# Attention of two layers: copies ahead of exponentials, plain outputs scaled once per token tile, five selection rounds moved

## The chip, the cores and the metric

The program runs on one core of one Trainium2 chip, as one launch. The metric is the device time of one execution in microseconds (us). Five engines work side by side, each with its own queue of instructions and joined only by semaphores: TensorE (PE; its weight loads are listed as PEld), VectorE (DVE), ScalarE (ACT), GpSimd (POOL) and the DMA queues, here those of SyncE (SP) and of ACT.

## The reference, cut to what matters

The program computes one state-space and mixture-of-experts block and then two layers of the following form on 512 tokens of width 1024. The change touches only the attention inside these two layers.

```python
for layer in range(2):
    h = rms_norm(x, g_mix[layer])
    qa, ka, va, iq, ik, iw, qb, kb, vb = split(h @ w_in[layer])
    out_a = dsa_mixer(qa, ka, va, iq, ik, iw)      # "plain": softmax over the keys that an index picks
    out_b = diff_mixer(qb, kb, vb, lam, ...)       # "differential": softmax 1 - lam * softmax 2, then a norm
    x = x + concat(out_a, out_b) @ w_out[layer]
    x = x + (silu(h2 @ w_gate) * (h2 @ w_up)) @ w_down     # h2 = rms_norm(x, g_ffn)
```

`dsa_mixer` has 8 heads of 64 values. For each query the index scores the keys and the best 128 of them are kept: a round finds the 8 largest scores of each row (`max`) and takes them out (`match_replace`), so a tile of 128 queries needs 16 rounds. `diff_mixer` has 4 heads with two score matrices each and 128 values.

## The kernel before, in words

**Units.** The attention of a layer is 32 units, `UNITS = [(i, h, d) for d in (1, 0) for i in range(4) for h in range(4)]`. Units 0 to 15 are differential (diff) and 16 to 31 plain; `i` is the tile of 128 queries and `h` a head (diff) or a pair of heads (plain). Tile `i` sees `128 * (i + 1)` keys, so the units grow with `i`: units 0 to 3 and 16 to 19 have 128 keys, 12 to 15 and 28 to 31 have 512. Each unit has two score matrices, c = 0 and 1.

**The pipeline of a unit u.** `qk` (PE, L3334) writes both score matrices to banks 2(u%2) and 2(u%2)+1 of PSUM. `top` (DVE, L3440) adds the mask, takes the negative row maximum and writes them to `Pb[u % 4]`. The exponentials (ACT, L3390) work in place on `Pb`. `normal` (DVE) divides: a diff unit by a reciprocal and two `scalar_tensor_tensor` (L3452 to L3457) into one matrix, a plain unit by a reciprocal and two `tensor_scalar` (L3459, L3461, L3462). `tr` (PE, L3344) transposes the 128x128 pieces into banks 4 and 5, ACT copies them to `PTb[u % 4]` (L3399), `pv` (PE, L3354 diff, L3359 plain) multiplies by the values into bank 6 + u%2, and ACT copies the result out (L3405): diff to `ob`, tokens on partitions; plain straight into `ym`, features on partitions, because there the values are the stationary operand with 64 columns and the transposed probabilities move.

**Order of work.** No planner is used: each engine runs a hand-written loop over steps s. PE at step s issues qk(s), tr(s-3), pv(s-4). ACT issues exp(s), copy(s-3), out(s-4). DVE issues top(s), at most one item of the rest of the key choice, normal(s-2), and some extras. The rest of the key choice is 17 items of the list `IDX`: a `bias` of tile 2 at s = 0, 15 rounds of tile 3 at s = 1 to 15, the `bias` of tile 3 at s = 16 (`index_dve`, rounds L3258 and L3260, bias L3262 to L3266). The bias of tile 3 is read first by top(28). Extras of DVE: `squares` of tile 0 to 3 at s = 21 to 24 (with the sums `n_sum` at 24), two splits of weights at s = 25 and 26 (L2942), a reciprocal at s = 27, the scaling of `ob` at s = 28 to 31 (L3502). Extras of ACT: two splits at s = 17 and 18 (L2938), the square root for the norm at s = 25 (L3412), which loads a function table and makes the next exponential load its own again.

**What waits.** qk(u) waits for top(u-2), tr(u) for normal(u) and for copy(u-1), pv(u) for copy(u) and for out(u-2), top(u) for qk(u) and tr(u-4).

**The end.** PE transposes `ob` into banks 0 to 3 at s = 33 and 34 (L3374) and ACT scales and copies it into `ym[4:8]` (`rows_T`, L3383). Then for k = 0 to 7 ACT rounds `ym[k]` to `hx[0]` (L3420) and DVE writes the remainder to `hx[1]` (L3505); ahead of k = 4 ACT splits one more weight item. The output projection (`lout_pe`, products at L296 to L298) takes its 1024 rows in pairs kp = 0 to 3 for the first half of columns; pair kp waits for the remainders of k = 2kp and 2kp+1. The load of the ring slot that holds `ym` waits for the remainder of k = 7 (`layers_sp`). After that PE runs through the output projection and the feed-forward part.

## Time and profile before

| what | before |
|---|---|
| runs, us | 3008.04, 3013.76, 3015.8 |
| median, us | 3013.76 |
| profiled execution: its time, us | 3006.61 |
| profiled execution: span in the trace, us | 3004.5 |
| mean granted clock of PE | 0.962 |
| attention, layer 0: first top to first product of the output projection | 1785.54 to 1892.75 us |
| attention, layer 1: the same | 2480.30 to 2586.05 us |

The profiled execution's own time is 2.1 us above its span. Times of rows are from the start of the span. The granted clock is 1.00 at 2.4 GHz and 0.50 at 1.2 GHz. The busy time of a row can overlap the next one by some ten nanoseconds, so that the cost of an instruction in a full queue is the distance from its start to the next start. An `[idle before <-X]` at the end of a row is the time for which the engine sat idle and what released it. An `xN` merges N instructions in a row; a 32-bit matmul is listed as two passes, a transpose as one.

### The profile page before, as it was taken

Reading aid. Unit: us, or ns where it says so; the run is one execution under the profiler, and the core shown is the slowest. Engines: PE = TensorE matmul, PEld = TensorE weight load, DVE = VectorE, ACT = ScalarE, POOL = GpSimd, SP = SyncE. Lnnn points to the kernel's source line nnn. Section 1 sums busy time; section 2 is a strip of 40 time slices with the busy share of each in tenths; the row PEclk is TensorE's granted clock in tenths of the full one; section 3 lists DMA queues with packets and bytes.
Section 4 is the critical chain, followed back from the end, with each engine's and each line's share of the span. In section 5 each row is a group of like instructions: output and inputs, shape, how many; then the busy total and the mean of one; then the engine's idle time right before and its main releaser. Section 6 shows DMA issues by size and latency. Waiting matters only on the chain.

```text
span 3004.5 us, 41883 instructions
## 1 busy us (share of the span) xinstructions
PE 2773.1 (92%) x16866; PEld 2113.7 (70%) x16866; DVE 1781.0 (59%) x3266; ACT 1137.6 (38%) x2028; POOL 152.4 (5%) x139
## 2 busy tenths in 40 slices
PE   7998977888999999999988987999999996899998
PEld 4887765776666676666645764788888774788887
DVE  4257866665777777766646698433333589443333
ACT  3322233222155655556523336432223336532222
POOL 0000000000012221222200000000000000000000
PEclk9998888989999999999999989999999998999999
DMA  6210001414269888999975320223313320222412
GB/s 226 85 57 22 1 1 48 123 53 154 98 245 355 337 346 328 343 358 348 361 291 206 106 97 1 86 90 107 110 67 121 110 103 8 85 70 78 140 53 74
DMA packets 186541, 442.37 MB, mean 147 GB/s; under 512 B 21283, under 2 KB 110694, under 8 KB 167014
## 3 DMA queue, kind: packets, MB, share of 16 engines
q1 hardware_dynamic: 161862, 396.59, 36.7%
q0 software_dynamic: 18720, 33.60, 2.9%
q10 hardware_dynamic: 5760, 9.44, 0.9%
q8 instruction: 136, 2.23, 0.3%
q14 instruction: 63, 0.52, 0.1%
HBM read 426.43 MB, written 38.29 MB: 155 GB/s over the span
## 4 chain that ended last, share of the span: by engine, by line
PE 65%; DVE 10%; DMA 6%; ACT 3%; issue 2%; POOL 0%; ACTq 0%; SPq 0%; POOLq 0%; DVEq 0%
PE ps L296 15%; PE ps L298 15%; PE ps L297 15%; PE ps L2496 5%; DMA ring<-in_ew 3%; DMA hg<-h_rows,idx 2%; PE ps L2012 2%; PE ps L1504 2%; DVE Pb L3440 1%; PE ps L2522 1%; PE ps L2735 1%; PE ps L2216 1%; DVE bi L3260 1%; DMA yr<-y_rows 1%; PE ps L3359 1%
## 5 line engine op out<-in xcount | busy, mean ns | idle before, releaser
L2942 DVE TENSOR_TENSOR wf<-ring,wf 128x1024 fp32r<-128x1024 f32 (+1 forms) x152 | 181.6, 1196 | 310.2 <-ACT wf L2938 309.9
L2938 ACT ACTIVATE wf<-ring 128x1024 fp32r<-128x1024 f32 (+1 forms) x152 | 156.8, 1033 | 342.9 <-PE ps L298 342.9
L296 PE MATMUL ps<-hxh,wf 128*128 128x512 f32 (+1 forms) x736 | 279.9, 380 | 2.3 <-DVE hxl L3089 2.3
L297 PE MATMUL ps<-hxl,wf 128*128 128x512 f32 (+1 forms) x736 | 279.5, 380 | 0.0
L298 PE MATMUL ps<-hxh,wf 128*128 128x512 f32 (+1 forms) x736 | 279.5, 380 | 0.0
L2434 DVE TENSOR_TENSOR spA<-ring,spA 128x1024 fp32r<-128x1024 f32 x156 | 184.4, 1221 | 103.8 <-ACT spA L2429 103.6
L2496 PE MATMUL ps<-ring,hdT 128*128 128x512 f32 x520 | 236.7, 598 | 0.8 <-issue 0.8
L2429 ACT ACTIVATE spA<-ring 128x1024 fp32r<-128x1024 f32 x156 | 157.9, 1054 | 50.5 <-DMA ring<-in_ew 44.3
L2434 DVE TENSOR_TENSOR spB<-ring,spB 128x1024 fp32r<-128x1024 f32 x104 | 124.1, 1220 | 69.3 <-ACT spB L2429 69.1
L2496 PEld LDWEIGHTS ps<-ring,hdT 128*128 128x128 f32 x520 | 94.5, 192 | 95.5 <-issue 92.0
L296 PEld LDWEIGHTS ps<-hxh,wf 128*128 128x128 f32 x736 | 138.4, 188 | 29.0 <-DVE hxl L3089 2.8
L297 PEld LDWEIGHTS ps<-hxl,wf 128*128 128x128 f32 x736 | 138.4, 188 | 26.2
L298 PEld LDWEIGHTS ps<-hxh,wf 128*128 128x128 f32 x736 | 138.4, 188 | 25.9
L296 PE MATMUL ps<-wf,hhh 128*128 128x512 f32 x352 | 137.0, 389 | 0.0
L298 PE MATMUL ps<-wf,hhl 128*128 128x512 f32 x352 | 136.9, 389 | 0.0
L297 PE MATMUL ps<-wf,hhh 128*128 128x512 f32 x352 | 136.9, 389 | 0.0
L296 PE MATMUL ps<-hxh,wr 128*128 128x512 f32 (+1 forms) x320 | 125.4, 392 | 10.6 <-DVE wr L2942 7.4
L296 PE MATMUL ps<-spA,hgT 128*128 128x512 f32 x312 | 126.7, 406 | 2.3 <-DVE hgT L2570 2.3
L298 PE MATMUL ps<-hxh,wr 128*128 128x512 f32 (+1 forms) x320 | 125.7, 393 | 0.0
L297 PE MATMUL ps<-hxl,wr 128*128 128x512 f32 (+1 forms) x320 | 124.3, 389 | 0.0
L2429 ACT ACTIVATE spB<-ring 128x1024 fp32r<-128x1024 f32 x104 | 106.5, 1052 | 46.5 <-DMA ring<-in_ew 36.4
L297 PE MATMUL ps<-spA,hgT 128*128 128x512 f32 x312 | 123.7, 396 | 0.0
(616 smaller groups left out, 6161.4 us busy)
## 6 DMA issues: line engine op xcount, KB each, us to landing
ring<-in_ew SPq DMA_DIRECT2D x65, 2048.0 KB, 12.1
ring<-in_ew SPq DMA_DIRECT2D x65, 1024.0 KB, 6.7
ring<-in_w_in SPq DMA_DIRECT2D x17, 2048.0 KB, 7.9
ring<-in_w_gate SPq DMA_DIRECT2D x20, 1024.0 KB, 5.4
ring<-in_w_up SPq DMA_DIRECT2D x20, 1024.0 KB, 8.0
ring<-in_w_down SPq DMA_DIRECT2D x16, 1024.0 KB, 5.1
adaw<-in_ada_w SPq DMA_DIRECT2D x24, 512.0 KB, 6.3
ring<-in_w_out SPq DMA_DIRECT2D x6, 2048.0 KB, 9.7
```

Source lines behind the costliest of these rows:

```text
L296: pe.matmul(o, lhs[0], rhs[0], start=start, stop=False)
L297: pe.matmul(o, lhs[0], rhs[1], start=False, stop=False)
L298: return pe.matmul(o, lhs[1], rhs[0], start=False, stop=stop)
L1504: m = pe.matmul(o[half(c), 64 * h:64 * h + 64], l[half(c), 64 * h:64 * h + 64], r[half(c), 64 * h:64 * h + 64])
L2012: m = pe.matmul(ps[2 * (i % 2) + hf][:, :], ym[:, k, i * 128:(i + 1) * 128], wv[:, k, :], start=(k == 0), stop=(k == 5))
L2216: m = pe.matmul(b[:, t], sw13[:, k, 256 * q + f * 128:256 * q + f * 128 + 128], hT[:, k, t], start=(k == 0), stop=(k == 7))
L2429: act.activation(piece(e, j)[0], piece_raw(e, j), ACT.Copy).then_inc(*p_hi.inc((e, j)))
L2434: v.tensor_tensor(piece(e, j)[1], piece_raw(e, j), f(piece(e, j)[0]), ALU.subtract).then_inc(*p_lo.inc((e, j)))
L2496: m = pe.matmul(ps[5 + q][:, :], hdT[:, n % 2, j, :], w2[:, j, q * 512:(q + 1) * 512], start=(j == 0), stop=(j == 1))
L2522: m = pe.transpose(ps[q][:, j * 128:(j + 1) * 128], hg[:, n % 3, (q * 4 + j) * 128:(q * 4 + j + 1) * 128], ident)
L2938: act.activation(item_part(n)[0], item_raw(n), ACT.Copy).then_inc(*w_hi.inc(n))
L2942: v.tensor_tensor(item_part(n)[1], item_raw(n), f(item_part(n)[0]), ALU.subtract).then_inc(*w_lo.inc(n))
```

## The change

Four things are altered in the attention of both layers.

1. **Order on ACT.** At step s ACT issues copy(s-2), out(s-4), exp(s) in place of exp(s), copy(s-3), out(s-4). On DVE normal(s-1) takes the place of normal(s-2). PE keeps qk(s), tr(s-3), pv(s-4), with tr of a plain unit waiting for its exponentials alone.
2. **Plain outputs.** The plain probabilities are no longer divided. `normal` of a plain unit is one reciprocal, kept in a new tile `rin`. `pv` of a plain unit has the transposed probabilities (128 columns) as stationary operand and moves 64 columns of values; the four units of a token tile fill one bank, 6 + i%2, tokens on partitions. Once per tile DVE multiplies the bank by the reciprocals into `r1` (`plain_norm`), PE transposes four pieces back into the bank (`plain_T`), and ACT copies it to `ym[0:4]` (`plain_y`). The 16 copies of plain units (L3405) go. The first `pv` of tile i waits for the bank: for out(14 + i) if i < 2, else for `plain_y(i - 2)`.
3. **Key choice.** The 17 items are issued at the steps marked in `REST`: the bias of tile 2 at 0, rounds at 1 to 6, 8, 10, 12, 14 (10) and at 16 to 20 (5), the bias of tile 3 at 26.
4. **The end.** The rounding to `hx` goes in the order k = 4 to 7, then 0 to 3 (`YK`), and the first half of the output projection takes its pairs in the order 2, 3, 0, 1 (`KP`). The third weight split stands ahead of k = 0. Tile 3's `plain_norm`, `plain_T`, `plain_y` come after the loop.

```diff
+            rin = sb("rin", [128, 16, 2], c=s1)
...
+    KP = ((2, 3, 0, 1), (0, 1, 2, 3))
+    YK = (4, 5, 6, 7, 0, 1, 2, 3)
...
+    REST = [int(s in (0, 1, 2, 3, 4, 5, 6, 8, 10, 12, 14, 16, 17, 18, 19, 20, 26)) for s in range(34)]
...
             if m == 9:
-                sp.wait_ge(*y_lo.val((l, 7)))
+                sp.wait_ge(*y_lo.val((l, YK[7])))
...
         def tr(u):
-            pe.wait_ge(*u_nrm.val((l, u)))
+            pe.wait_ge(*(u_nrm if diff else u_exp).val((l, u)))
...
         def pv(u):
-            if u >= 2:
+            if diff and u >= 2:
                 pe.wait_ge(*u_out.val((l, u - 2)))
+            if not diff and h == 0:
+                pe.wait_ge(*(u_out.val((l, 14 + i)) if i < 2 else q_y.val((l, i - 2))))
...
-                        m = pe.matmul(ps[6 + u % 2][64 * c:64 * c + 64, 0:128], vt[:, j, 128 * h + 64 * c:128 * h + 64 * c + 64],
-                                      PTb[:, u % 4, c, j * 128:(j + 1) * 128], start=(j == 0), stop=(j == i))
+                        m = pe.matmul(ps[6 + i % 2][:, 128 * h + 64 * c:128 * h + 64 * c + 64], PTb[:, u % 4, c, j * 128:(j + 1) * 128],
+                                      vt[:, j, 128 * h + 64 * c:128 * h + 64 * c + 64], start=(j == 0), stop=(j == i))
+
+        def plain_T(i):
+            pe.wait_ge(*q_n.val((l, i)))
+            for h in range(4):
+                m = pe.transpose(ps[6 + i % 2][:, 128 * h:128 * h + 128], r1[:, i % 2, h * 128:(h + 1) * 128], ident)
+            m.then_inc(*q_T.inc((l, i)))
...
+            if s in (25, 29, 33):
+                plain_T((s - 25) // 4)
...
+        plain_T(3)
...
+        def plain_y(i):
+            act.wait_ge(*q_T.val((l, i)))
+            act.activation(ym_(l)[:, 0:4, i * 128:(i + 1) * 128], v4(ps[6 + i % 2][:, :]), ACT.Copy).then_inc(*q_y.inc((l, i)))
         for s in range(36):
+            if 2 <= s < 34:
+                i, h, diff = UNITS[s - 2]
+                act.wait_ge(*u_tr.val((l, s - 2)))
+                if s >= 6:
+                    act.wait_ge(*u_pv.val((l, s - 6)))
+                for c in range(1 if diff else 2):
+                    m = act.activation(PTb[:, (s - 2) % 4, c, 0:128 * (i + 1)], ps[4 + c][:, 0:128 * (i + 1)], ACT.Copy)
+                m.then_inc(*u_pt.inc((l, s - 2)))
+            if 4 <= s < 20:
+                act.wait_ge(*u_pv.val((l, s - 4)))
+                act.activation(ob[:, i, 128 * h:128 * h + 128], ps[6 + s % 2][:, 0:128], ACT.Copy).then_inc(*u_out.inc((l, s - 4)))
...
+            if s in (26, 30, 34):
+                plain_y((s - 26) // 4)
...
-        act.wait_ge(*u_out.val((l, 31)))
-        for k in range(8):
-            if k == 4:
-                act.wait_ge(*n_y.val((l, 3)))
+        rows_T(2)
+        act.wait_ge(*n_y.val((l, 3)))
+        for k in YK:
+            if k == 0:
+                act.wait_ge(*q_y.val((l, 3)))
                 split_hi(act, n0 + 2)
             act.activation(hx[0][:, k, :], ym_(l)[:, k, :], ACT.Copy).then_inc(*y_hi.inc((l, k)))
-            if k == 1:
-                rows_T(2)
+            if k == 5:
+                plain_y(3)
...
-                v.reciprocal(s_[:, 6:8], s_[:, 4:6]).then_inc(*V.inc())
-                v.wait_ge(*V.val())
-                v.tensor_scalar(p0, p0, s_[:, 6:7], None, ALU.mult).then_inc(*V.inc())
-                v.tensor_scalar(p1, p1, s_[:, 7:8], None, ALU.mult).then_inc(*u_nrm.inc((l, u)))
+                v.reciprocal(rin[:, u - 16, :], s_[:, 4:6]).then_inc(*u_nrm.inc((l, u)))
...
+        def plain_norm(i):
+            v.wait_ge(*u_pv.val((l, 19 + 4 * i)))
+            v.wait_ge(*u_nrm.val((l, 19 + 4 * i)))
+            if i >= 2:
+                v.wait_ge(*q_T.val((l, i - 2)))
+            v.tensor_tensor(r1[:, i % 2, :].rearrange("p (n q) -> p n q", q=64), ps[6 + i % 2][:, :].rearrange("p (n q) -> p n q", q=64),
+                            bc(rin[:, 4 * i:4 * i + 4, :].rearrange("p h c -> p (h c)"), 64), ALU.mult).then_inc(*q_n.inc((l, i)))
...
-            for x in rest[s:s + 1]:
+            for x in rest[at:at + REST[s]]:
                 index_dve(v, l, x)
-            if s >= 2:
-                normal(s - 2)
+            at += REST[s]
+            if 1 <= s < 33:
+                normal(s - 1)
...
+            if s in (24, 28, 32):
+                plain_norm((s - 24) // 4)
...
+        plain_norm(3)
+        for k in YK:
             v.wait_ge(*y_hi.val((l, k)))
...
+            for at, kp in enumerate(KP[hf][0:4 - 2 * hf]):
+                n = n0 + 4 * hf + at
```

## Rows read from the trace of the kernel before

**Rows 1.** Windows: us, busy us (instructions) of PE, PEld, DVE, ACT, POOL; clock; DMA.

```profile
1850.32:1892.75 42.43, 32.32 (x256) 22.39 (x257) 25.35 (x85) 29.09 (x77) 0.00 (x0) 0.96 0.00 1
2480.30:2527.80 47.50, 29.45 (x138) 16.75 (x136) 45.82 (x155) 24.85 (x89) 0.00 (x0) 0.75 0.04 12
2527.80:2545.20 17.40, 13.86 (x104) 9.44 (x104) 14.04 (x83) 13.82 (x54) 0.00 (x0) 1.00 0.01 2
2545.20:2586.05 40.85, 30.75 (x257) 21.76 (x257) 25.35 (x85) 28.92 (x77) 0.00 (x0) 1.00 0.00 1
```

**Rows 2.** Timeline, DVE, layer 1: start us, busy us, line, tiles, [idle before].

```profile
2520.35 0.68 DVE L3440 CUSTOM_DVE_ANT_0 Pb<-ps,zb 128x512 f32<-128x512 f32 x1
...
2521.57 0.69 DVE L3258 MAX8 m8b<-bi 128x8 f32<-128x512 f32 x1
...
2522.97 0.15 DVE L3452 RECIPROCAL stt<-stt 128x1 f32<-128x1 f32 x1
...
2524.08 0.68 DVE L3440 CUSTOM_DVE_ANT_0 Pb<-ps,zb 128x512 f32<-128x512 f32 x1
...
2528.22 0.42 DVE L3262 TENSOR_SCALAR bi<-bi 128x512 f32<-128x512 f32 x1
...
2529.32 0.16 DVE L3452 RECIPROCAL stt<-stt 128x1 f32<-128x1 f32 x1
```

**Rows 3.** Timeline, ACT, layer 1: around the square root, later units, the end.

```profile
2551.45 1.28 ACT L3412 ACT_TABLE_LOAD   x1
...
2554.36 0.61 ACT L3390 ACTIVATE Pb<-Pb,stt 128x384 f32<-128x384 f32 x1
...
2555.58 0.63 ACT L3399 ACTIVATE PTb<-ps 128x256 f32<-128x256 f32 x2
...
2560.24 0.72 ACT L3390 ACTIVATE Pb<-Pb,stt 128x512 f32<-128x512 f32 x1 [1.75 <-DVE stt L3440]
...
2561.67 0.84 ACT L3399 ACTIVATE PTb<-ps 128x384 f32<-128x384 f32 x2
...
2583.99 1.15 ACT L3420 ACTIVATE hxh<-ring 128x512 fp32r<-128x512 f32 x2
2585.05 1.25 ACT L3383 ACTIVATE ring<-ps,gsc 128x512 f32<-128x512 f32 x2
```

**Rows 4.** Timeline, DVE, layer 1, plain units.

```profile
2558.90 0.69 DVE L3440 CUSTOM_DVE_ANT_0 Pb<-ps,bi 128x512 f32<-128x512 f32 x1 [2.52 <-PE ps L3334]
...
2570.05 0.49 DVE L3461 TENSOR_SCALAR Pb<-Pb,stt 128x512 f32<-128x512 f32 x1
...
2570.85 0.68 DVE L3502 TENSOR_TENSOR ob<-ob,nrm 128x512 f32<-128x512 f32 x1
```

**Rows 5.** Groups by line and form, DVE, plain part of layer 1: busy us, mean ns.

```profile
L3472 DVE CUSTOM_DVE_ANT_0 nsq<-ob 128x128 f32<-128x128 f32 x16 | 3.7, 286 | 0.0
...
L3461 DVE TENSOR_SCALAR Pb<-Pb,stt 128x128 f32<-128x128 f32 x4 | 1.1, 286 | 0.1
```

**Rows 6.** Timeline, PE, layer 1.

```profile
2531.07 1.06 PE L3354 MATMUL ps<-vt,PTb 128*128 128x128 f32 x8
...
2557.72 1.13 PE L3334 MATMUL ps<-qT 64*128 64x512 f32 x4
2558.78 0.87 PE L3344 MATMUL ps<-csb,Pb 128*128 128x128 f32 x6
2559.59 1.14 PE L3359 MATMUL ps<-PTb,vt 128*64 128x128 f32 x12
...
2576.13 1.58 PE L3359 MATMUL ps<-PTb,vt 128*64 128x128 f32 x16
2577.64 1.09 PE L3374 MATMUL ps<-csb,ob 128*128 128x128 f32 x8
...
2586.05 0.47 PE L296 MATMUL ps<-wf,hxh 128*128 128x512 f32 x1 [2.40 <-issue]
```

**Rows 7.** Window of layer 0 inside the diff part, columns as in rows 1.

```profile
1804.00:1807.00 3.00, 2.77 (x12) 1.40 (x9) 2.90 (x11) 1.33 (x7) 0.00 (x0) 0.50 0.00 0
```

More of the change, by code:

```diff
@@ L382, in _program @@
     a_ada = Signal(sem("ada_mm"), range(4))
-    a_row = Signal(sem("ada_copy"), range(4))
-    a_rT = Signal(sem("ada_T"), range(2))
-    a_mod = Signal(sem("modc_set"), range(2))
+    a_row = Signal(sem("rows_copy"), range(4))
+    a_rT = Signal(sem("rows_T"), range(2))
+    a_mod = Signal(sem("rows_set"), range(2))
     SEGS = ((1, slice(0, 256)), (0, slice(256, 768)))
@@ L2884, in _program @@
         for hf in range(2):
-            add([krows(WO[:, hf * 512:(hf + 1) * 512])], 8, [("out", 0, A2[kp], slice(0, 512)) for kp in range(4)])
+            add([krows(WO[:, hf * 512:(hf + 1) * 512])], 8, [("out", 0, A2[kp], slice(0, 512)) for kp in KP[hf]])
         for grp in range(2):
@@ L2976, in _program @@
     u_pv = Signal(sem("unit_pv"), UL)
-    u_out = Signal(sem("unit_out"), UL)
+    u_out = Signal(sem("unit_out"), [(l, u) for l in range(2) for u in range(16)])
     i_mm = Signal(sem("index_mm"), IG)
@@ L2987, in _program @@
     lam_e = Signal(sem("lam_exp"), ["set"])
-    y_hi = Signal(sem("y_hi"), [(l, k) for l in range(2) for k in range(8)])
-    y_lo = Signal(sem("y_lo"), [(l, k) for l in range(2) for k in range(8)])
+    y_hi = Signal(sem("y_hi"), [(l, k) for l in range(2) for k in YK])
+    y_lo = Signal(sem("y_lo"), [(l, k) for l in range(2) for k in YK])
+    q_n = Signal(sem("rows_set"), [(l, i) for l in range(2) for i in range(4)])
+    q_T = Signal(sem("rows_T"), [(l, i) for l in range(2) for i in range(4)])
+    q_y = Signal(sem("rows_copy"), [(l, i) for l in range(2) for i in range(4)])
     o_tile = Signal(sem("tile_mm"), [(l, k, i) for l in range(2) for k in ("out", "ff") for i in range(3)])
@@ L3502, in attn_dve @@
                 v.tensor_tensor(v4(ob[:, i, :]), v4(ob[:, i, :]), bc(nrm[:, 0, 4 * i:4 * i + 4], 128), ALU.mult).then_inc(*n_mul.inc((l, i)))
-        for k in range(8):
+        plain_norm(3)
+        for k in YK:
             v.wait_ge(*y_hi.val((l, k)))
             v.tensor_tensor(hx[1][:, k, :], ym_(l)[:, k, :], f(hx[0][:, k, :]), ALU.subtract).then_inc(*y_lo.inc((l, k)))
-            if k == 3:
+            if k == 7:
                 split_lo(v, n0 + 2)
@@ L3514, in part @@
             for k in range(2):
-                kk, w = 2 * kp + k, item_part(n0 + 4 * hf + kp)
+                kk, w = 2 * kp + k, item_part(n0 + 4 * hf + KP[hf].index(kp))
                 m = mm3(pe, ps[4 * hf + i][:, :], [x[:, kk, i * 128:(i + 1) * 128] for x in hx], [x[:, k, :] for x in w],
-                        start=(kk == 0), stop=(kk == 7))
+                        start=(kk == 2 * KP[hf][0]), stop=(kk == 2 * KP[hf][3] + 1))
             return m
         for hf in range(2):
-            for kp in range(4 - 2 * hf):
-                n = n0 + 4 * hf + kp
+            for at, kp in enumerate(KP[hf][0:4 - 2 * hf]):
+                n = n0 + 4 * hf + at
                 pe.wait_ge(*w_lo.val(n))
@@ L3525, in lout_pe @@
                 for i in range(4):
-                    if hf == 0 and kp == 0:
+                    if hf == 0 and at == 0:
                         pe.wait_ge(*n_y.val((l, i)))
```

15 lines of the change are left out of this document (2 added, 13 removed).

## The prediction

> **What bounds the kernel now.** I read the windows first, cut at three marks: the first `top`, `top` of unit 16, `top` of unit 24, and the first product of the output projection. That gives part A (diff), B (plain, tiles 0 and 1) and C (plain, tiles 2 and 3, and the end). [rows 1] show A at 47.50 us with DVE busy for 45.82, so DVE alone sets A. In B (17.40 us) DVE is busy for 14.04 and in C (40.85) for 25.35, with PE at 30.75 and ACT at 28.92: there nobody is full and the engines wait for each other. Layer 0 has the same A and B and a C of 42.43. Behind C the PE products follow each other without a gap for most of the layer, so an earlier start of the output projection is an earlier end.
>
> The timelines then give the prices. In a full queue a price is the distance between starts; where only a busy time stands it is some 0.07 less. On DVE, at 512 keys [rows 2]: `top` 1.22, a round 1.40, `normal` of a diff unit 1.11, the bias of tile 3 1.10. A plain pair of multiplications costs 0.80 at 512 keys [rows 4] and, as 2 x 0.286 less overlap, 0.41 at 128 [rows 5]; 0.54 at 256 lies on the line. On ACT [rows 3]: two exponentials 1.22 at 384 keys and 1.43 at 512; two copies of transposes 0.55 at 256, 0.76 at 384 and so 0.95 at 512; a full-width copy 0.53 to 0.62; the square root with its two table loads 2.91. On PE [rows 6]: `qk` 1.06 at 512 keys; 6 transposes 0.81, 8 about 1.0; plain `pv` 1.07 at 384 keys (12 passes), 1.51 at 512 (16 passes). Waits: DVE sat 2.52 in front of top(28) [rows 4], behind the square root; ACT 1.75 in front of exp(28) [rows 3]; PE 2.40 before the output projection [rows 6], while ACT copied, rounded, and DVE took remainders.
>
> **Part A.** Of the 15 rounds ten stay and five leave: 5 x 1.40 = 7.0. normal(14) comes in, since `normal` runs one step earlier: + 1.1. Net 5.9 off, 41.6 left, if DVE stays the bound. A step without a round costs DVE 1.22 + 1.11 = 2.33 at 512 keys. Against that stand ACT with 1.43 + 0.48 + 0.17 = 2.1 and PE with 1.06 + 0.5 + 0.99 = 2.55 (`pv` 8 passes, [rows 6]); but steps with and without a round alternate, so DVE needs 3.0 on average. The longest circle that the new order makes is top, qk two steps on, tr, copy, exp, normal, top: 1.2 + 1.1 + 0.5 + 0.7 + 1.4 + 1.1 and some 0.5 of hand-overs, 6.5 in three steps, 2.2 a step. It is hidden.
>
> **Part B.** The diff part shows how full a full DVE queue looks: 45.82 / 47.50 = 0.965. So the 14.04 busy us of B are 14.5 of queue, and 2.9 were waiting [rows 1]. Out: the bias 1.1, normal(14) 1.1, six pairs of multiplications 4 x 0.41 + 2 x 0.54 = 2.7. In: five rounds 7.0, one more reciprocal 0.2. Sum 14.5 - 4.9 + 7.2 = 16.8. The 2.9 of waiting goes, because those waits were for PE held up by `copy`, and copy now stands ahead of exp; ACT and PE have some 14 us of work here. B falls by 0.6.
>
> **Part C**, as a timetable with t = 0 at top(24). DVE: top 1.0, squares 4 x 0.21 [rows 5] with three small sums 1.5, `plain_norm(0)` 0.6: done at 3.2. `plain_norm` has no row; the nearest is the 512-wide multiplication of L3502 with 0.68 busy, 0.60 in the queue [rows 4]. PE has reached `plain_T(0)` by then and waits in front of it, with qk(26) and tr(23) queued behind: transposes 0.5, qk 0.85, tr(23) 0.55, done at 5.1. This is the new wait. ACT holds exp(25) behind copy(23), so exp(25) ends at 7.0, square root and table loads 2.9, copy(24) 0.75, exp(26) 1.2: 11.8. `plain_y(0)` 0.6 ends at 12.4. DVE meanwhile does top(25), a split, top(26), the bias, a split, top(27) and waits some 2 us for exp(26); top(28) comes at 12.5. pv(24) is held by plain_y(0), its bank being in use, until 12.4; from there PE is full. Its list: pv(24) 1.07; three steps of qk, tr and pv, 1.06 + 0.81 + 1.07 each, of which the last has 8 transposes, + 0.2, and `plain_T(1)` 0.5: 9.5; tr(29), pv(28) 2.5; tr(30), pv(29), plain_T(2), eight transposes 4.0; tr(31), pv(30), eight transposes 3.5; pv(31) 1.5. Together 22.1, and one stall of 1.1: pv(28) needs plain_y(1), which stands behind copy(28) and exp(30). pv(31) ends at about 35.5. Then plain_norm(3) 0.7, and DVE's remainders of k = 4 and 5, 2 x 0.6, which alone keep the projection back; transposes and plain_y(3) go beside them. First product at 37.5. Against 40.85 that is 3.3 off in layer 1, and against 42.43, 4.9 in layer 0, where before one stretch ran at 0.96 of the clock.
>
> The other halves of the edit cost nothing on this path. The copies of 16 plain units (0.17 each) go off ACT. Pairs kp = 3, 0, 1 have 5.4 us of products each between them, and ACT's third split and the rest of the rounding need less. The ring load behind the last remainder moves with it. Should this cover fail, each late pair costs what it is late.
>
> **One price is unknown:** a pass with 128 stationary and 64 moving columns. 128 and 128 cost (1.06 - 0.07) / 8 = 0.124, 64 and 128 cost 1.51 / 16 = 0.094 [rows 6]. `qk` shows what moving columns cost: 1.06 / 4 = 0.265 at 512, and a straight line from 0.124 at 128 gives 0.03 for 64. So 0.124 - 0.03 = 0.094: no change, the value I take. Its bounds are 0.124 (moving fewer columns gives nothing) and 0.064 (the larger weight load costs nothing). PE is the bound for 112 passes of units 24 to 31 in each layer, so that is +-6.7 us over both layers. The Trainium skill ("TensorE: Matmul & The Clock Gate", section "LDWEIGHTS (loading the stationary operand)") has the load cost its columns at 1.2 GHz, 53 ns for the 64 added, which speaks against the swap: 0.094 + 0.053 - 0.03 = 0.117, + 5.2 us by an estimate from that page. The trace has the step from 64 to 128 stationary columns at 0.030, not 0.053.
>
> **Sum.** Layer 1: 5.9 + 0.6 + 3.3 = 9.8. Layer 0: 5.9 + 0.6 + 4.9 = 11.4. Together 21.2. The profiled execution took 3006.6 us, 2.1 above its span, and should take 2985.4. The median of the runs is 7.2 above that execution, and I keep this distance: 3013.8 - 21.2 = 2992.6.
>
> **Rivals.**
> 1. *The swapped product is dearer,* 0.124 a pass at worst. For it: no row has that form, and C is bound by PE. Against it: the line through its neighbours gives 0.094. Gain 21.2 - 6.7 = 14.5, time 2999. The page of the Trainium skill named above speaks for this rival, and would have it at 2998.
> 2. *Handing over eats it.* With DVE, ACT and PE all near 34 us in the 16 plain steps, any unevenness is a stall; the 2.9 of B come back and C loses as much again in waits such as plain_T in front of qk. Gain 21.2 - 2 x 5 = 11, time 3003. For it: C has both a filled PE and two waits of plain work on ACT. Against it: copy ahead of exp takes out the wait that ended most steps.
> 3. *PE at the lower clock becomes the bound of A.* A runs at 0.75 mean clock [rows 1], and at 0.50 PE was busy for 2.77 of 3.00 us just before the clock rose [rows 7]. With rounds gone, steps of tile 2 and 3 at 1.2 GHz need 3.2 and 4.4 to 5.0 of PE against 2.6 and 3.0 of DVE. If the clock stayed low to unit 16: + 8 a layer, gain 5, time 3009, no change by measure.
> 4. *The other side: the low clock lasts into the plain part.* Same place and mechanism. At 1.2 GHz a plain step of tiles 0 and 1 needs 2.7 to 3.8 of PE against about 2.1, 8 to 10 us in B, on top of rival 3. It decides once over 11 us of a layer's PE work that would have run at 2.4 GHz and is on the path runs at 1.2 beyond what did before: gain 5 - 18, time 3027. Against it: before, the clock rose as soon as PE had filled its queue, and the change fills it more.
> 5. *The load behind the remainders hides it:* no; PE waited for no weights in the feed-forward part.
>
> **How the numbers follow.** My forecast (gain 17 to 27) 0.58; rival 1 0.12; rival 2 0.16; rival 3 0.06; rival 4 0.04; better than that, by a cheap pass or better clock, 0.04. A measurement of this kernel tells 0.3%, 9 us, from no change. Faster: 0.58 + 0.12 + 0.12 of rival 2 + 0.04 = 0.86; same: the other 0.04 of rival 2 and 0.05 of rival 3; slower: 0.01 of rival 3 and 0.04 of rival 4. The range 2986 to 3003 takes in the forecast, rival 1 and half of rival 2.
>
> **What would show it.** A near 41.6 with DVE busy at 0.96 of it; B near 16.8 with no idle row over 0.5 at `top`; C near 37.5 in both layers; passes of L3359's successor near 0.094; PE full from pv(24) with about 1 us in front of pv(28); 0.7 to 1 us in front of the output projection. I am wrong if idle time appears on DVE in A, if PE waits for `plain_y` by more than named, if top(28) comes later than 13 behind top(24), or if the granted clock is 0.50 past unit 11.

## The result, and the profile after

Over six runs of each, side by side on one chip, the changed kernel's median is 2995.58 us (2987.31 to 2999.16) and that of the kernel before 3010.43 us (3006.31 to 3015.8). The ratio is 0.9945, its 95% interval 0.993 to 0.9959: faster by 0.55%. The forecast was 2992.6 us and a gain of 21.2; the medians give 14.9, the ratio 16.6. The direction and the range held. The gain is 5 to 6 us short, and the parts show where. That the time itself came within 3.0 us of the forecast is in part luck: the median of the kernel before, from which the forecast subtracts, is 3.3 us lower in these six runs than the 3013.76 that it started from.

| part, us | layer 0: forecast | before | after | layer 1: forecast | before | after |
|---|---|---|---|---|---|---|
| A: top(0) to top(16) | 41.6 | 47.37 | 41.57 | 41.6 | 47.50 | 41.56 |
| B: top(16) to top(24) | 16.8 | 17.41 | 15.49 | 16.8 | 17.40 | 15.60 |
| C: top(24) to the output projection | 37.5 | 42.43 | 41.07 | 37.5 | 40.85 | 42.49 |
| sum | 95.9 | 107.21 | 98.13 | 95.9 | 105.75 | 99.65 |

The table is from one profiled execution of each kernel. Together the two layers gain 9.08 + 6.10 = 15.2 us. The profiled execution of the changed kernel has a span of 2996.0 us, only 8.5 below that of before. The rest is ahead of the change: its first `top` starts at 1791.71 us, that of before at 1785.54, with the same code up to there. Over the profiles of this study that start lies between 1779.71 and 1791.71. So spans are not compared below, only the parts of the attention.

The windows of the changed kernel, A and B of layer 1, C of layer 0 and C of layer 1 (columns as in [rows 1]):

```profile
1848.77:1889.84 41.07, 35.66 (x261) 28.62 (x261) 21.13 (x71) 28.44 (x70) 0.00 (x0) 0.96 0.00 1
2476.30:2517.86 41.56, 30.30 (x154) 17.82 (x152) 40.02 (x142) 24.79 (x89) 0.00 (x0) 0.78 0.05 13
2517.86:2533.46 15.60, 13.51 (x102) 10.53 (x104) 15.34 (x83) 13.43 (x51) 0.00 (x0) 1.00 0.01 2
2533.46:2575.95 42.49, 36.98 (x261) 29.88 (x259) 21.09 (x71) 28.33 (x70) 0.00 (x0) 0.92 0.00 1
```

DVE is busy for 0.963 of A, about as before the change (0.965), and now for 0.98 of B. It has no idle row in either part. In C the granted clock is 0.96 in layer 0 and 0.92 in layer 1, against 0.96 and 1.00 in [rows 1].

The timeline of PE in C of layer 1 (it answers to [rows 6]) holds the shortfall:

```profile
2543.15 0.84 PE L3351 MATMUL ps<-csb,Pb 128*128 128x128 f32 x6
2546.24 2.79 PE L3368 MATMUL ps<-vt,PTb 128*128 128x64 f32 x12 [2.25 <-ACT ring L3404]
2548.97 2.08 PE L3341 MATMUL ps<-qT 64*128 64x512 f32 x4
2550.98 1.54 PE L3351 MATMUL ps<-csb,Pb 128*128 128x128 f32 x6
2552.31 1.65 PE L3368 MATMUL ps<-vt,PTb 128*128 128x64 f32 x12
2553.80 0.61 PE L3375 MATMUL ps<-csb,r 128*128 128x128 f32 x4
2554.34 1.13 PE L3341 MATMUL ps<-qT 64*128 64x512 f32 x4
2555.40 0.87 PE L3351 MATMUL ps<-csb,Pb 128*128 128x128 f32 x6
2556.11 1.45 PE L3368 MATMUL ps<-vt,PTb 128*128 128x64 f32 x12
2557.49 1.13 PE L3341 MATMUL ps<-qT 64*128 64x512 f32 x4
...
2562.80 1.97 PE L3368 MATMUL ps<-vt,PTb 128*128 128x64 f32 x16 [0.83 <-ACT ring L3404]
...
2565.48 1.90 PE L3368 MATMUL ps<-vt,PTb 128*128 128x64 f32 x16
2567.22 0.60 PE L3375 MATMUL ps<-csb,r 128*128 128x128 f32 x4
...
2575.95 0.47 PE L296 MATMUL ps<-wf,hxh 128*128 128x512 f32 x1 [0.59 <-issue]
```

L3368 is the new plain `pv`. From start to next start sixteen passes take 2567.22 - 2565.48 = 1.74 (1.73 in other rows), that is 0.108 to 0.109, and twelve 1.38, that is 0.115. The idle row is pv(24), 12.78 us behind top(24), and it waits for `plain_y(0)` (L3404) on ACT. What follows it runs at half speed: `qk` is listed with 2.08 where it has 1.13 a few rows on, and twelve passes take 2.73 in place of 1.38.

The timeline of ACT just before (it answers to [rows 3]) shows why `plain_y(0)` is late:

```profile
2540.64 1.28 ACT L3434 ACT_TABLE_LOAD   x1
2541.93 0.31 ACT L3434 ACTIVATE nrm<-nrm,eps 128x16 f32<-128x16 f32 x1
2542.15 0.85 ACT L3412 ACTIVATE PTb<-ps 128x384 f32<-128x384 f32 x2
2543.02 1.28 ACT L3423 ACT_TABLE_LOAD   x1
2544.31 0.61 ACT L3423 ACTIVATE Pb<-Pb,stt 128x384 f32<-128x384 f32 x1
...
2545.53 0.58 ACT L3404 ACTIVATE ring<-ps 128x512 f32<-128x512 f32 x1
```

Its input, the four transposes of `plain_T(0)`, started at 2536.64 us and took 0.66, so it had been ready for 8.2 us. It stands in ACT's queue behind exp(26), which stands behind the square root and two table loads.

### The profile page after: what moved, and what is told of

The parts are those of the page before. It is cut to its first block, busy times and chain, and to the rows that moved or that the text cites. A ratio compares the mean times of both kernels' runs of the same rounds, so it can differ in the third digit from the quotient of the medians.

```text
span 2996.0 us, 41851 instructions
## 1 busy us (share of the span) xinstructions
PE 2791.6 (93%) x16898; PEld 2135.4 (71%) x16898; DVE 1764.9 (59%) x3210; ACT 1136.5 (38%) x2004; POOL 151.2 (5%) x139
## 4 chain that ended last, share of the span: by engine, by line
PE 68%; DVE 8%; DMA 5%; ACT 2%; issue 2%; POOL 0%; ACTq 0%; SPq 0%; POOLq 0%; DVEq 0%
PE ps L296 15%; PE ps L298 15%; PE ps L297 15%; PE ps L2496 6%; DMA hg<-h_rows,idx 2%; PE ps L2012 2%; DMA ring<-in_ew 2%; PE ps L1504 2%; PE ps L2522 2%; DVE Pb L3463 1%; PE ps L2735 1%; PE ps L2216 1%; PE ps L3368 1%; DVE bi L3267 1%; DMA yr<-y_rows 1%
## 5 line engine op out<-in xcount | busy, mean ns | idle before, releaser
L2429 ACT ACTIVATE spA<-ring 128x1024 fp32r<-128x1024 f32 x156 | 157.9, 1054 | 50.6 <-DMA ring<-in_ew 41.6
L296 PE MATMUL ps<-spA,hgT 128*128 128x512 f32 x312 | 127.1, 407 | 2.6 <-DVE hgT L2570 2.6
L298 PE MATMUL ps<-spA,hgT 128*128 128x512 f32 x312 | 124.4, 399 | 0.0
L297 PE MATMUL ps<-spA,hgT 128*128 128x512 f32 x312 | 124.3, 398 | 0.0
```

The source lines that it names most:

```text
L296: pe.matmul(o, lhs[0], rhs[0], start=start, stop=False)
L297: pe.matmul(o, lhs[0], rhs[1], start=False, stop=False)
L298: return pe.matmul(o, lhs[1], rhs[0], start=False, stop=stop)
L2429: act.activation(piece(e, j)[0], piece_raw(e, j), ACT.Copy).then_inc(*p_hi.inc((e, j)))
```

## The experiments

Each edit is made on the changed kernel, but for the one that says otherwise. Parts in us, layer 0 / layer 1, from one profiled execution each; the ratio is to the kernel before, in the same session, with its 95% interval.

| kernel | A | B | C | ratio |
|---|---|---|---|---|
| changed | 41.57 / 41.56 | 15.49 / 15.60 | 41.07 / 42.49 | 0.9945 (0.993 to 0.9959) |
| plain_y early | 41.56 / 41.57 | 15.49 / 15.59 | 36.59 / 36.58 | 0.9912 (0.9894 to 0.993) |
| gap filled | 41.57 / 41.57 | 15.48 / 15.60 | 40.78 / 40.77 | 0.993 (0.9909 to 0.9951) |
| part 2 undone | 41.57 / 41.55 | 19.90 / 19.60 | 35.95 / 35.23 | 0.9942 (0.9922 to 0.9963) |
| part 3 undone | 48.50 / 48.49 | 15.87 / 14.93 | 39.44 / 41.06 | 0.9981 (0.9966 to 0.9995) |
| part 4 undone | 41.56 / 41.54 | 15.50 / 15.60 | 41.56 / 44.63 | 0.9962 (0.9949 to 0.9976) |
| part 1 undone | 42.48 / 43.89 | 18.27 / 18.27 | 46.31 / 43.37 | 0.9992 (0.9982 to 1.0001) |
| part 3 alone, on before | 42.49 / 42.50 | 20.69 / 21.91 | 42.44 / 42.44 | 0.9989 (0.998 to 0.9999) |
| plain_y early, late root | 41.56 / 41.55 | 15.49 / 15.59 | 36.76 / 36.76 | 0.9913 (0.9898 to 0.9928) |
| plain_y early, again | 41.56 / 41.56 | 15.48 / 15.59 | 36.60 / 36.59 | 0.9915 (0.9898 to 0.9932) |
| and two rounds on | 38.77 / 38.77 | 15.65 / 15.49 | 36.60 / 36.59 | 0.9888 (0.9869 to 0.9906) |
| and norm first | 38.77 / 38.78 | 15.64 / 15.49 | 36.65 / 36.64 | 0.9888 (0.987 to 0.9906) |
| no rounds in A | 30.18 / 30.84 | 15.49 / 15.48 | 36.94 / 36.59 | one run, 2959.3 us |

### Is the late plain_y the cause of the long C?

```diff
                 m.then_inc(*u_pt.inc((l, s - 2)))
+            if s in (25, 29, 33):
+                plain_y((s - 25) // 4)
...
-            if s in (26, 30, 34):
-                plain_y((s - 26) // 4)
```

> Edit on the changed kernel: plain_y(i) is issued at s = 25, 29, 33 right behind the copy of transposes, ahead of that step's exponentials and of the square root, in place of s = 26, 30, 34 behind the exponentials. In the changed kernel part C takes 41.1 us in layer 0 and 42.5 in layer 1, against 37.5 forecast; PE idles 2.25 before the first plain product of tile 2 and then works at 1.2 GHz for some microseconds. Theory 1 (the wait for the bank and the clock that falls behind it): the wait of 2.25 and that of 0.83 before tile 3 go, the clock stays at 2.4 GHz, C falls to 37 to 38.5 in both layers, 7 to 9 us faster in all. Theory 2 (the dearer pass, 0.108 in place of 0.094, sets C, waits are slack): C falls by less than 1.5 in each layer. Theory 3 (the clock falls for another reason): the waits go, PE still has a stretch at 1.2 GHz, C falls by about 3 in each layer.

C falls to 36.6 in both layers, by 4.5 and 5.9 us. That is theory 1, and more than its 7 to 9 us in all. The windows and pv(24) in the timeline of PE, layer 1 of this kernel:

```profile
2516.97:2553.55 36.58, 33.50 (x261) 27.57 (x259) 20.92 (x71) 28.19 (x70) 0.00 (x0) 1.00 0.00 1
```

```profile
2527.13 0.85 PE L3351 MATMUL ps<-csb,Pb 128*128 128x128 f32 x6 [0.50 <-ACT PTb L3412]
2527.82 1.45 PE L3368 MATMUL ps<-vt,PTb 128*128 128x64 f32 x12
2529.20 1.13 PE L3341 MATMUL ps<-qT 64*128 64x512 f32 x4
```

pv(24) starts 10.85 us behind top(24), with no wait of its own, and PE has the full clock all through C. The stall before pv(28) is gone too. Run a second time, beside other kernels, it gave the same parts to 0.01 us.

> The kernel with the early plain_y alone once more, beside the three others on the same chip: the parts are 41.6, 15.6 and 36.6 us again in both layers, and the ratio to the kernel before is 0.990 to 0.993.

### The wait or the clock?

The gap before pv(24) can cost in two ways, by its length and by the clock behind it. Here the gap is filled with eight passes of `qk` whose result nobody reads.

```diff
+                if i == 2:
+                    pe.wait_ge(*u_max.val((l, 27)))
+                    for k in range(4):
+                        pe.matmul(ps[2][:, :], qT[0:64, 0, 0:128], qT[0:64, 4, :])
                 pe.wait_ge(*(u_out.val((l, 14 + i)) if i < 2 else q_y.val((l, i - 2))))
```

> Edit on the changed kernel: ahead of the wait of pv(24) for its bank PE does four extra 64x128 by 512 products, about 2.1 us at 2.4 GHz, into a free bank that is written again later; their result is not used. The wait for plain_y(0) stays. Theory 1, the part on the clock: PE no longer idles, the granted clock stays 1.00, so pv(24) still starts 12.8 us behind top(24), but C ends 1.5 us earlier in layer 0 and 3 to 3.5 earlier in layer 1. If the idle time of 2.25 us is not what lowers the clock: C is the same within 0.5 us, with the same stretch at 1.2 GHz.

Timeline of PE, layer 1:

```profile
2541.43 3.70 PE L3363 MATMUL ps<-qT 64*128 64x512 f32 x8
2545.05 1.55 PE L3372 MATMUL ps<-vt,PTb 128*128 128x64 f32 x12
2546.53 1.13 PE L3341 MATMUL ps<-qT 64*128 64x512 f32 x4
```

The filling takes 3.6 us, longer than the gap and than the 2.1 expected (0.45 a pass at a clock of 1.00, where a pass of `qk` takes 0.265; why was not tried). So pv(24) starts 14.1 us behind top(24), 1.3 later than in the changed kernel. Yet C is shorter, by 0.3 us in layer 0 and 1.7 in layer 1, and the clock stays at 1.00. So the low clock alone cost 0.3 + 1.3 = 1.6 us in layer 0 and 1.7 + 1.3 = 3.0 in layer 1, and without the idle time it did not come. That idle time does not always bring it is seen below, in the old end.

### The plain outputs as they were (part 2 undone)

```diff
-            pe.wait_ge(*(u_nrm if diff else u_exp).val((l, u)))
+            pe.wait_ge(*u_nrm.val((l, u)))
...
-                        m = pe.matmul(ps[6 + i % 2][:, 128 * h + 64 * c:128 * h + 64 * c + 64], PTb[:, u % 4, c, j * 128:(j + 1) * 128],
-                                      vt[:, j, 128 * h + 64 * c:128 * h + 64 * c + 64], start=(j == 0), stop=(j == i))
+                        m = pe.matmul(ps[6 + u % 2][64 * c:64 * c + 64, 0:128], vt[:, j, 128 * h + 64 * c:128 * h + 64 * c + 64],
+                                      PTb[:, u % 4, c, j * 128:(j + 1) * 128], start=(j == 0), stop=(j == i))
...
```

The divisions on DVE and the 16 copies of plain outputs are back, and `plain_norm`, `plain_T` and `plain_y` are gone.

> Part 2 of the change undone: plain probabilities are divided by VectorE, values are the stationary operand with 64 columns, plain outputs are copied unit by unit, no plain_norm, plain_T, plain_y. Order, rounds and end as in the changed kernel. If the plain outputs are worth what they take off DVE (pairs 0.41 to 0.80 in 16 units, 9.6 us, less four plain_norm of 0.6): B is longer by 2.5 to 3.5 than 15.5, C longer by 2 to 4 than if its clock stayed high, so the kernel is some 6 to 10 us slower than the changed one. If, as the rival has it, the dearer pass (2.2 us a layer), 16 more transposes on PE and the wait for the bank with its clock dip cancel that: C is 39 to 41 in both layers, and the kernel within 4 us of the changed one.

B is 4.4 and 4.0 us longer, C 5.1 and 7.3 shorter, their sum 0.7 and 3.3 shorter than in the changed kernel. So the new plain outputs, with `plain_y` where the change put it, cost 4 us net over both layers. The low clock behind the gap, 4.6 us over both layers, is more than all of that: C of this kernel has no gap over 1.1 us ahead of its end and a clock of 1.00. With `plain_y` a step earlier the same outputs gain: 187.4 for both layers against 193.8. By the intervals of their ratios this kernel and the changed one do not differ; the parts do.

### The rounds back in A (part 3 undone)

```diff
-    REST = [int(s in (0, 1, 2, 3, 4, 5, 6, 8, 10, 12, 14, 16, 17, 18, 19, 20, 26)) for s in range(34)]
+    REST = [int(s < 17) for s in range(34)]
```

> Part 3 of the change undone: 17 items of the key choice at steps 0 to 16. Theory of the prediction (DVE alone bounds A): A is 41.6 + 7.0 = 48.6 us, B is 15.5 - 7.0 + 1.1 if DVE stayed the bound, but PE and ACT then bound it, so 12.5 to 14; C loses the bias of 1.1 in step 26. Net 3 to 5 us slower in each layer. Rival (rounds moved are only moved, DVE is as full in B): no difference.

A is 48.5, 6.9 us longer, which is five rounds of 1.39. B hardly moves (+0.4, -0.7), though it has lost five rounds, 7 us of DVE, and got only the bias, 1.1: DVE now sits idle for 5.5 and 4.7 us of B, mostly in wait for exponentials, and those are the waits that the rounds fill. In layer 0 B also ran at a clock of 0.88 and is 0.9 us longer than in layer 1, where it ran at 1.00.

C is 1.6 and 1.4 shorter, and that is the clock, not the rounds. The gap of 2.25 us before pv(24) stands in both layers as in the changed kernel. Behind it the clock stays at 1.00 in layer 0 and falls in layer 1, for 1.6 us, where in the changed kernel it fell for 1.6 and 3.0.

### The old end (part 4 undone)

```diff
-    KP = ((2, 3, 0, 1), (0, 1, 2, 3))
-    YK = (4, 5, 6, 7, 0, 1, 2, 3)
+    KP = ((0, 1, 2, 3), (0, 1, 2, 3))
+    YK = (0, 1, 2, 3, 4, 5, 6, 7)
...
```

On ACT `plain_y(3)` stands ahead of all rounding again.

> Part 4 alone undone: the rounding and the pairs of the output projection go in the order 0 to 7 and 0 to 3 again, tile 3's plain_y stands ahead of all rounding. Parts A and B as in the changed kernel (41.6 and 15.5 us). Theory, part 4 takes the plain work of tile 3 off the path: before the projection PE now waits for plain_norm 0.6, plain_T 0.5, plain_y 0.6 and two roundings and remainders 1.2 in a row, 2.9 in place of 0.6, so C is 2 to 2.5 us longer in each layer, some 4.5 us in all. Rival, the end is set by pv(31) and the remainders alone and the order is worth nothing: C changes by less than 0.5 us.

Timeline of PE, layer 1, at the end of C:

```profile
2570.30 0.66 PE L3375 MATMUL ps<-csb,r 128*128 128x128 f32 x4 [0.79 <-DVE r L3507]
2573.68 0.77 PE L296 MATMUL ps<-wf,hxh 128*128 128x512 f32 x1 [2.72 <-issue]
```

The idle time before the projection is 2.72 in place of 0.59, the 2.1 us that the theory asks for, and C of layer 1 is 2.14 longer. In both layers part 4 is worth the same; C of layer 0 is only 0.5 longer because there the clock gave the rest back. Timeline of PE, C of layer 0 of this kernel:

```profile
1855.95 1.52 PE L3368 MATMUL ps<-vt,PTb 128*128 128x64 f32 x12 [2.25 <-ACT ring L3404]
1857.40 1.13 PE L3341 MATMUL ps<-qT 64*128 64x512 f32 x4
```

The gap before pv(24) is 2.25 us as in the changed kernel, yet `qk` behind it takes 1.13: no 1.6 us of low clock here, so that 2.1 - 1.6 = 0.5 is left.

### The old order on ACT (part 1 undone)

```diff
-            if 1 <= s < 33:
-                normal(s - 1)
+            if s >= 2:
+                normal(s - 2)
```

and on ACT exp(s), copy(s-3), out(s-4) again.

> Part 1 alone undone: ACT issues exp(s), copy(s-3), out(s-4) again and DVE normal(s-2). Theory, copy ahead of exp is what makes B better than forecast and keeps the diff part on DVE: A loses normal(14) and is 1.1 shorter (40.5), B gets that 1.1 back and waits of up to 2.9 us (17 to 19.5), and C is longer by 1 to 3 us; sum of A, B and C 2 to 4 us longer in each layer. Rival, the order on ACT does not matter once the multiplications of plain units are gone: A -1.1, B +1.1, sum within 0.5 us.

A should have lost normal(14) and come to 40.5. It came to 42.5 and 43.9. B is 2.7 longer, C 5.2 and 0.9, and the ratio is that of no change. In C the two layers differ by the clock: behind a gap of 2.46 us it was at 0.50 for ten us in layer 0, and at 0.56 and 0.58 in two windows of 2 us in layer 1. The waits of part A, layer 1, in the timeline of DVE and then in that of PE:

```profile
2504.78 0.56 DVE L3463 CUSTOM_DVE_ANT_0 Pb<-ps,zb 128x384 f32<-128x384 f32 x1 [1.26 <-PE ps L3341]
...
2511.30 0.56 DVE L3463 CUSTOM_DVE_ANT_0 Pb<-ps,zb 128x384 f32<-128x384 f32 x1 [1.42 <-PE ps L3341]
...
2516.87 0.69 DVE L3463 CUSTOM_DVE_ANT_0 Pb<-ps,zb 128x512 f32<-128x512 f32 x1 [0.22 <-PE ps L3341]
```

```profile
2502.04 0.69 PE L3351 MATMUL ps<-csb,Pb 128*128 128x128 f32 x2 [0.86 <-DVE Pb L3480]
...
2503.08 1.65 PE L3341 MATMUL ps<-qT 64*128 64x384 f32 x4
...
2514.77 0.55 PE L3351 MATMUL ps<-csb,Pb 128*128 128x128 f32 x3 [1.61 <-DVE Pb L3480]
...
2515.69 1.13 PE L3341 MATMUL ps<-qT 64*128 64x512 f32 x4
```

`top` waits for `qk`, `qk` stands on PE behind `tr` and `pv`, and `tr` waits for `normal` (L3480), which in the old order ends only just ahead of the `top` before. So tr, pv and qk have to fit into one step of DVE. With a round in every step they do, and the circle does not show. Without a round a step of DVE is 1.9 to 2.3 us. At full clock the three just fail to fit, and `top` waits 0.22. The two long waits of 1.26 and 1.42 fall where the granted clock was still 0.50 (2503.08 to 2511.30): there the three take 0.48 + 1.00 + 1.58 = 3.06. The second of them is missing in layer 0, where the clock rose 5 us earlier, and that is the 1.4 us between 42.5 and 43.9. With `normal` a step earlier, as in the changed kernel, `tr` has its input a step sooner, and DVE has no wait in A. In B it is another circle: plain `tr` waits for a copy on ACT (0.70 us in front of the `qk` for which `top` then waits 0.44). Which half of part 1 gives what, the order on ACT or the earlier `normal`, was not tried apart.

### The rounds alone (part 3 on the kernel before)

```diff
-            for x in rest[s:s + 1]:
+            for x in rest[at:at + REST[s]]:
                 index_dve(v, l, x)
+            at += REST[s]
```

`REST` is that of the changed kernel.

> Part 3 alone on the kernel before: five rounds and the bias of tile 3 leave part A for part B and C. A is 47.4 - 7.0 = 40.4 us. Theory, the old plain part has 3 us of waiting in B, which the rounds fill: B 17.4 + 5.9 (five rounds in, the bias out) - 2.9 = 20.4, C 1 us longer by the bias at most; gain 3 us in each layer, 6 in all. Rival, the rounds only move and the waits stay, since they are waits behind DVE's own work: B 23.3, C as before or longer, no gain within 1 us a layer.

A is 42.5, not 40.4: 2.1 us of the 7.0 stay. The waits at `top` are those of the old order, 1.26 at a clock of 0.50 and then 0.22 and 0.17, in both layers. B and C take most of the rest: the sum is 105.62 in layer 0 (1.6 less than before) and 106.85 in layer 1 (1.1 more). The clock has a share in that too. It was 0.92 and 0.81 in B, against 1.00 before, and behind the gap of 2.88 us in C it fell in both layers, for about 1.7 us each by the windows, where before it fell in layer 0 alone. Neither theory is right in full. The rounds alone bring little; with part 1 they bring their price.

### Is ACT's square root on the path?

```diff
-            if s == 25:
+            if s == 32:
                 act.wait_ge(*n_sum.val(l))
```

with the early plain_y, and the four scalings on DVE at step 33, the transposes of the diff outputs at 34 and 35.

> plain_y one step early, ahead of the copy that follows, as in the earlier experiment, and in addition the square root of the norm moved from step 25 to step 32, behind the last exponential, with the scaling of the outputs on DVE in one piece at step 33. Both function table loads leave the middle of the plain part, 2.9 us of ACT in each layer; one of them, 1.3 us, should vanish, since the norm behind the attention can use the table that is loaded. Theory A, ACT's 2.9 us are on the path of part C: C is 33.5 to 34.5 us in place of 36.6, and the whole is 4 to 7 us below the experiment with the early plain_y alone. Theory B, PE is full there and ACT's 2.9 us are slack: C stays within 1 us of 36.6, or is longer because scaling and transposes of the diff outputs now stand at the end, and only the 1.3 us of a table load behind the projection are won, 2.6 us or nothing.

Theory B. C is 36.76, 0.2 longer. pv(24) starts 10.30 us behind top(24) in place of 10.85, so the two table loads had cost 0.5 us there, once `plain_y` did not stand behind them. PE ends its last `pv` 1.6 us earlier, half of that because eight transposes now come after it, and waits 2.39 before the projection in place of 0.59. What the saved table load gives behind the projection can't be told: that stretch is 419.0 us here and 419.9 with the early plain_y alone, but lies between 418.4 and 420.9 over the profiles of this study. The ratio equals that of the early plain_y alone.

### Is A still DVE's alone?

```diff
-    REST = [int(s in (0, 1, 2, 3, 4, 5, 6, 8, 10, 12, 14, 16, 17, 18, 19, 20, 26)) for s in range(34)]
+    REST = [(0, 1, 2, 3, 4, 5, 6, 8, 10, 16, 17, 18, 19, 20, 25, 26, 26).count(s) for s in range(34)]
```

> The early plain_y, and two more rounds of the key choice moved, from steps 12 and 14 to steps 25 and 26, where DVE waits for exponentials (2.69 us idle in one row). Theory, A is still set by DVE alone: A 41.57 - 2 x 1.39 = 38.8 us, B unchanged at 15.6, C at most 0.5 us longer; 2.3 to 2.8 us less in each layer than with the early plain_y alone. Rival, A without those rounds is set by PE at half clock or by the circle over ACT: A falls by less than 1 us, and C grows by what top(28) comes later, no gain.

A is 38.77, 2.80 less, and C is the same to 0.01: two rounds went into DVE's waits for exponentials (0.52 and 2.69 with the early plain_y, 0.28 here) for nothing. This is the best of the kernels, 0.9888, and better than both that the study began with.

```profile
2465.97:2504.74 38.77, 30.77 (x152) 18.31 (x152) 37.30 (x137) 24.71 (x89) 0.00 (x0) 0.74 0.04 14
```

This is A of layer 1. DVE is busy for 0.96 of it, as before the change and after.

Last, A with no round of its own. This kernel leaves ten of the fifteen rounds out and so picks other keys; it only shows what A costs.

```diff
-            for x in rest[at:at + REST[s]]:
+            for x in rest[at:at + REST[s] * (s < 1 or s > 14)]:
```

> The early plain_y, and the ten rounds of the key choice that stand in part A left out altogether, so that tile 3's choice is made by six rounds in place of sixteen. It shows what the diff part costs when DVE is not its bound. If DVE still set it, A would be 41.6 - 13.9 = 27.7 us. By the third rival of the prediction PE at half clock takes over in tiles 2 and 3, 3.2 and 4.4 to 5.0 us a step: A 33 to 36 us with the granted clock at 0.50 for its most part. If PE is filled and gets full clock, A is 28 to 30 us.

A is 30.18 and 30.84 where DVE alone would need 27.7. PE does take over for a time, but the clock rises with it. The windows of layer 1's A in three pieces:

```profile
2455.83:2466.00 10.17, 9.01 (x34) 5.03 (x34) 8.30 (x46) 6.68 (x30) 0.00 (x0) 0.50 0.14 50
2466.00:2476.00 10.00, 10.00 (x53) 5.70 (x52) 8.45 (x34) 8.15 (x30) 0.00 (x0) 0.87 0.01 2
2476.00:2486.67 10.67, 10.07 (x69) 6.81 (x67) 10.31 (x35) 9.74 (x31) 0.00 (x0) 1.00 0.00 0
```

In the first piece the clock is at its lower level, 1.2 GHz, and PE busy for 0.89. Then it rises, and in the last piece DVE (10.31 of 10.67) is again the busiest. Fewer rounds in A do not strand PE at half clock.

### Is every wait of PE in C worth its length?

On the kernel with two more rounds moved:

> As the kernel with two more rounds moved, and in addition the plain_norm of a tile ahead of the squares of the same step on DVE, so that plain_T(0), at which PE waited 1.04 us, finds its input there. Theory, every microsecond of PE in C counts: C 0.7 to 1 us shorter in each layer. Rival, the wait was slack, since PE waits for a copy behind exponentials before pv(24) anyway: C within 0.3 us.

```diff
-            if 21 <= s < 25:
-                squares(s - 21)
             if s in (24, 28, 32):
                 plain_norm((s - 24) // 4)
+            if 21 <= s < 25:
+                squares(s - 21)
```

The wait of 0.94 to 1.04 at `plain_T(0)` is gone, and C does not move (36.65 and 36.64). The wait has only a new name. Timeline of PE, layer 1, qk(29):

```profile
2534.04 1.13 PE L3341 MATMUL ps<-qT 64*128 64x512 f32 x4 [1.34 <-DVE stt L3463]
```

Without the edit qk(29) starts at the same place, 12.45 us behind top(24) against 12.49, and waits 0.15. Up to there PE is held by the chain of tops, exponentials and copies, and a microsecond given to it is waited out at qk(29).

## Why the prediction was right, and by how much it was off

**What bounds the kernel** was read right: DVE sets A, and nobody sets B and C alone. A came out at 41.57 against 41.6, from 5 rounds out and one `normal` in. That it stays DVE's with two rounds fewer still (38.77) shows that the price was right and not two errors that cancel. The circle of 2.2 us a step that I called hidden is hidden in the new order. The old order has another one, over `normal`, tr, pv and qk, which would have eaten 2.0 to 3.4 us of A, most of it at half clock.

**Part B**, 16.8 forecast, is 15.5 to 15.6. Two terms were off. The waits: the four idle rows at `top` sum to 2.87 us in the kernel before, but an instruction that waits also loses the 0.07 by which it would overlap the row ahead of it. So waiting was 3.15 and the queue 14.25 of the 17.40, not 14.5. The reciprocals: I put one more in, at 0.2. In the timeline of DVE, layer 1, of the kernel before and of the changed one:

```profile
2533.02 0.16 DVE L3459 RECIPROCAL stt<-stt 128x2 f32<-128x2 f32 x1
2533.22 0.29 DVE L3461 TENSOR_SCALAR Pb<-Pb,stt 128x128 f32<-128x128 f32 x1
...
2522.60 0.16 DVE L3482 RECIPROCAL rin<-stt 128x2 f32<-128x2 f32 x1
2522.68 0.27 DVE L3463 CUSTOM_DVE_ANT_0 Pb<-ps,zb 128x128 f32<-128x128 f32 x1
```

A reciprocal whose result the next instruction waits for costs 0.20, and one whose result it does not need 0.08. B had six of the first kind, 1.15 us, and has seven of the second, 0.52: 0.6 less where I had 0.2 more. These are 0.25 and 0.8 of the 1.2 us. That the waits go because copy stands ahead of exp fits the kernel without part 1 (B 18.27, of which 1.1 us are waits at `top` and 1.1 is normal(14)).

**Part C**, 37.5 forecast, is 41.07 and 42.49. For layer 1 the 5.0 us are, from the timeline above:

- *the unknown pass*: 1.38 us for twelve and 1.74 for sixteen, where the timetable had 1.07 and 1.5, so that eight `pv` of units 24 to 31 are 2.3 us longer. The transposes around them are shorter, 0.71 for six and about 0.9 for eight in place of 0.81 and 1.0, and give 0.7 back: 1.6 net, as much as 0.108 in place of 0.094 makes over 112 passes. That lies between the value taken and the upper bound of 0.124. The mechanism (fewer columns to move, a larger load) was right, the two sizes were not, and the working shows why below.
- *the clock behind the gap*: pv(24) 2.73 in place of 1.38, `qk` 2.01 for 1.06, six transposes 1.33 for 0.71, pv(25) 1.49 for 1.38: 3.0 us. In layer 0 the same four rows give 1.6. The filled gap gives the same two numbers. This is the step that failed, the larger one in layer 1: I had the gap in the timetable (pv(24) "until 12.4") and wrote "from there PE is full", but priced what follows at full clock.
- pv(24) 0.4 later, the stall before pv(28) 0.83 for 1.1, the end 0.2 longer: + 0.3.

That is 4.9 of 5.0.

The pass was priced from unlike rows: 128 and 128 columns from a group of 8 passes, 64 and 128 from a group of 16. The price of a pass depends on the group. At eight passes each, from start to next start, 64 and 128 cost 0.59 (2557.13 below, with the `qk` at 2557.72 of [rows 6] behind it), 128 and 128 cost 0.99 ([rows 6]), and 128 and 64 cost 0.94:

```profile
2538.57 1.00 PE L3368 MATMUL ps<-vt,PTb 128*128 128x64 f32 x8
2539.51 0.92 PE L3341 MATMUL ps<-qT 64*128 64x384 f32 x4
```

So the larger load costs 0.050 a pass and not 0.030, and the 64 moving columns fewer give 0.006 and not the 0.03 of the straight line through `qk`. The value taken, 0.124 - 0.03, failed by that line. The prediction's sentence that the trace has the load's step at 0.030 rests on the unlike rows too.

The kernel before had the warning of the clock in it. I read layer 0's 42.43 against layer 1's 40.85 as one stretch at 0.96 and let the new kernel start without it. The timeline of PE of the kernel before, in C of layer 0 and then of layer 1:

```profile
1861.47 1.13 PE L3344 MATMUL ps<-csb,Pb 128*128 128x128 f32 x6 [2.88 <-ACT PTb L3399]
1862.53 1.13 PE L3359 MATMUL ps<-PTb,vt 128*64 128x128 f32 x8
1863.59 1.96 PE L3334 MATMUL ps<-qT 64*128 64x512 f32 x4
...
2556.35 0.85 PE L3344 MATMUL ps<-csb,Pb 128*128 128x128 f32 x6 [2.88 <-ACT PTb L3399]
2557.13 0.66 PE L3359 MATMUL ps<-PTb,vt 128*64 128x128 f32 x8
```

The same idle time of 2.88 us was followed by the low clock in one layer, for 1.6 us, and not in the other. The gap of 2.25 us was followed by 1.6 and 3.0 us in the changed kernel, by 0 and 3.0 in the one without part 4, and by 0 and 1.6 in the one without part 3. A new gap of that kind had to be entered with a cost between 0 and 3 us a layer, or taken out. Of the signs of being wrong that the prediction named, one came true: the clock was 0.50 past unit 11, for the 4 us behind the start of pv(24) in layer 1.

**The rivals.** Rival 1, the dearer pass, held in kind: 0.108 at sixteen passes, half of its price. Rival 2, that handing over eats it, held in place: `plain_y(0)` behind exp(26) is a wait of plain work on ACT, as it named; but it costs by the clock more than by the wait. The gain of 15.2 us lies between the forecast's 21.2 and its 11. Rival 3, PE at half clock as the bound of A, fell for the changed kernel: A is DVE's, and without any round in A, PE brings its clock up. In the old order it holds for one or two steps, the waits of 1.26 and 1.42. Rival 4 needed rival 3; the clock did come low into the plain part, in C and not in B, from an idle gap and not from a clock that never rose, and it cost 4.6 us over both layers, far from the point at which it decides. Rival 5 was right to be dropped: from the first product of layer 0's projection to the first `top` of layer 1 it is 587.6 us before and 586.5 after, so what the attention saves is kept.

**The end** went as forecast: 0.59 before the projection, `plain_norm(3)` in front of it, and the old end costs 2.1 more idle time.

**What the parts are worth.** Undone one at a time, part 1 costs 8.9 and 5.9 us a layer, part 3 5.7 and 4.8, part 4 0.5 and 2.1; part 2 undone gains 0.7 and 3.3. Part 3 alone is worth 1.6 and -1.1. So they don't add up: part 1 and the moved rounds pay only together, and part 2 only with its copy a step earlier.

These figures are from one profile each, and the low clock fell differently in each. With the clock's share taken out where the rows or windows give it, the estimates are, per layer: part 4 is worth 2.1 us in both, part 3 6.2 to 6.3, part 1 5.4 to 5.8, and part 2 with its late copy 0.9 and -0.3. The attention itself has gained 15.2 us with 4.6 us of low clock in C against 1.6 before. A difference of less than 3 us in C between two single profiles can be the clock alone.

**Open.** Why attention starts up to 12 us earlier or later from profile to profile, with equal code, was not tried. Nor was what decides whether a gap of 2 to 3 us is followed by the low clock, and for how long. Not shown either is why twelve passes cost 0.115 each and sixteen 0.108.
